# Two hybrid blocks on one core: first weight units split on VectorE, keys and queries by tile, squares of the post norms added on VectorE

## The chip, the cores and the metric

One core of one Trainium2 chip. The metric is the device time of one execution in microseconds (us); lower is better. Engines: PE (TensorE, matmuls), PEld (its weight loads), DVE (VectorE), ACT (ScalarE), POOL (GpSimd) and SP (SyncE, which here issues every DMA).

## What is computed

Two transformer-like blocks on a sequence of 512 tokens of width 1024, in f32, each with 16 meta tokens put in front. Reduced to what matters:

```python
def rmsnorm(x, g):
    return x * lax.rsqrt(jnp.mean(x * x, axis=-1, keepdims=True) + 1e-6) * g

# first block
mix = hybrid_mixer(rmsnorm(h, norm_mix_pre))      # retention + stick-breaking attention, gates, w_out
h = h + rmsnorm(mix, norm_mix_post)
h = h + rmsnorm(swiglu(rmsnorm(h, norm_ffn_pre)), norm_ffn_post)      # d_ff 2816
# second block
h = h + rmsnorm(mixer(rmsnorm(h, pre_mix_norm)), post_mix_norm)       # two convolutions, w_out
h = h + rmsnorm(swiglu_2(rmsnorm(h, pre_ffn_norm)), post_ffn_norm)
```

There are thus eight RMS norms, n = 0 to 7. The even ones (0, 2, 4, 6) are the norms ahead of a product, the odd ones (1, 3, 5, 7) the post norms.

## The kernel before, in words

**Layout.** Activations lie transposed: 8 tiles (k = 0 to 7) of 128 channels by 512 tokens, or 528 (FULL) with the meta tokens. Weights come in 140 units of 128x2048 f32 (1 MB), two buffers each of `w_raw`, `w_hi`, `w_lo`. For nearly f32 accuracy every operand is split in an fp32r part and a rest: ACT writes `w_hi` (a copy of `w_raw` to fp32r, `split_hi`, L872), DVE writes `w_lo` = `w_raw` - `w_hi` (`split_lo`, L1297), and each product is three matmuls (`mm3`, L477 to L481). A unit of kind P has 2 output strips of 8 tiles, R has 4 strips of 4, D has 8 strips of 2. A strip is a PSUM bank of 128x512; ACT or DVE takes it out and counts `strip_free`.

**Order of the work.** Each engine has one instruction stream, written out by hand, and waits on counting semaphores; there is no scheduler. SP issues the load of unit u when `w_hi` and `w_lo` of unit u-2 are there (`load`, L403). At the start it issues the four parts of h, unit 0, constants, unit 1, and the rotary table (L388 to L402). In w_out, the reload of h and `meta2` is issued ahead of the later units (L439, L440), once X_lo of the mixed rows is done.

**A norm (n)**: ACT squares the tiles into the two buffers of `sq` (`squares`, L907); PE sums over channels with a matmul by a matrix of ones, plain f32, into bank 6 (`sums`, L525 to L535), one per tile, each of them counted on `sq_added`; square k waits for sum k-2, since its buffer must be free; then ACT computes std as Ln and Exp (`norm`, L880). In a pre norm DVE then multiplies h by gain and std (`normed`, L1322), ACT writes X_hi, DVE X_lo (L1316; `norm_split`, L1309); in a post norm DVE makes `normed` from `acc` and adds it to h (`norm_add`, L1329).

- n = 1: phase w_out, 4 P units. PE puts two sums behind each of units 1, 2 and 3 and the last two at the end (`out_product`, L794). ACT splits the next weights (`split_hi`) ahead of the square of each odd tile (L1164); DVE copies each strip to `acc` and splits after each odd one (L1679).
- n = 3 and n = 7: phase ffn_end, one D unit. DVE adds each strip to `acc` (`add_up`, L1445); the 8 sums stand on PE behind the whole unit. With n = 3 ACT splits a weight unit ahead of the last square (L1206), and DVE makes its rest behind its last strip.
- n = 5: phase w_out2_b, two R units, sums behind both; ACT splits a unit ahead of squares 0 and 4 (L1282), DVE makes both rests behind its last strip.
- After most sums PE runs `keep_warm`: matmuls of ones by ones whose result nobody reads.

**The start.** PE: sums of norm 0, 36 matmuls of `keep_warm`, then `key_strip` (L568): the keys' strip of unit 0, tile by tile as X_lo comes, then 16 small matmuls for the meta tokens, then the queries' strip of the same unit (`unit(at, 0, 0, "P", SEQ, from_x, [1])`, L703). ACT copies unit 0 to `w_hi` between the second and third X_hi (`first_hi(0)`, L902), unit 1 after the small operands of the first quad (L1042). DVE makes the rest of unit 0 behind its second `normed` (L1324) and of unit 1 behind the norm. Then come K_hi and K_lo, the meta keys KM, Q_hi and Q_lo, and with these the first scores (L588).

## Time and profile before

| | |
|---|---|
| time, median of 3 runs | 2011.96 us (2009.48 to 2012.11) |
| time of the profiled execution | 2012.64 us |
| its span, first to last instruction | 2010.8 us |
| busy: PE / PEld / DVE / ACT / POOL | 1948.0 / 1644.5 / 1102.2 / 714.0 / 19.1 us |
| mean granted TensorE clock (share of 2.4 GHz) | 0.992 |
| weights and inputs read from HBM | 154.48 MB |

Busy time of PE is a model: matmuls are pipelined, so a matmul's duration is longer than its step, the distance from one start to the next. In a timeline, the time in square brackets is how long the engine had stood idle before an instruction, and who ended it. An f32 matmul appears as two records. L870 is the line of ACT's helper for every activation, so its instructions are told apart by their tiles; L1307 is the same for DVE's scalar_tensor_tensor.

### The profile page before, as it was taken

What the parts mean: (1) busy time and instruction counts of PE and PEld (TensorE: products, weight loads), DVE (VectorE), ACT (ScalarE), POOL (GpSimd) and SP (SyncE); (2) the same over time, 40 slices, a digit from 0 to 9 for tenths busy, and PEclk for the clock granted to TensorE, in tenths of its full rate; (3) what the DMA queues carried; (4) which work ended last, traced back from release to release, by engine and by line L of the source; (5) the groups of instructions that cost most, each with busy time, mean ns of one, the idle gap of its engine ahead of it and who ended that gap; (6) DMA issues with size and microseconds to landing.
All of it is one profiled execution on the core that took longest, in us unless ns stands there. A gap on an engine that the chain in (4) does not pass through costs nothing.

```text
span 2010.8 us, 25243 instructions
## 1 busy us (share of the span) xinstructions
PE 1948.0 (97%) x10194; PEld 1644.5 (82%) x10194; DVE 1102.2 (55%) x1354; ACT 714.0 (36%) x853; POOL 19.1 (1%) x16
## 2 busy tenths in 40 slices
PE   7999999899999999999999999999999999999996
PEld 6988989789888898978768888886998668888884
DVE  4556565542463736357364544546699664544545
ACT  5666666522323233233342222224333442222222
POOL 1000000000000000000000000000000000000000
PEclk9999999899999999999999999999999999999998
DMA  4011111032222121212412323222121112323221
GB/s 160 33 42 43 63 42 43 21 115 78 80 84 87 70 73 63 84 66 82 149 62 85 104 83 104 90 97 84 64 85 63 63 62 85 104 83 104 89 99 42
DMA packets 23474, 157.53 MB, mean 78 GB/s; under 512 B 2672, under 2 KB 3056, under 8 KB 5360
## 3 DMA queue, kind: packets, MB, share of 16 engines
q1 hardware_dynamic: 23408, 156.59, 22.5%
q8 instruction: 49, 0.80, 0.2%
q14 instruction: 17, 0.14, 0.0%
HBM read 154.48 MB, written 2.10 MB: 78 GB/s over the span
## 4 chain that ended last, share of the span: by engine, by line
PE 84%; DVE 8%; ACT 4%; issue 2%; DMA 1%; DVEq 0%; SPq 0%; ACTq 0%
PE psum L479 27%; PE psum L480 26%; PE psum L481 26%; PE psum L609 2%; PE psum L533 2%; DVE z L1307 2%; DVE normed L1307 2%; DVE h L1336 1%; ACT w_hi L870 1%; DVE w_lo L1300 1%; ACT std L870 1%; DMA w_raw<-in_units 0%; ACT sp L870 0%; PE psum L630 0%; ACT X_hi L870 0%
## 5 line engine op out<-in xcount | busy, mean ns | idle before, releaser
L479 PE MATMUL psum<-X_hi,w_hi 128*128 128x512 f32 (+1 forms) x1632 | 601.9, 369 | 5.9 <-DVE X_lo L1316 5.0
L481 PE MATMUL psum<-X_hi,w_lo 128*128 128x512 f32 (+1 forms) x1632 | 595.0, 365 | 0.0
L480 PE MATMUL psum<-X_lo,w_hi 128*128 128x512 f32 (+1 forms) x1632 | 594.9, 365 | 0.0
L870 ACT ACTIVATE w_hi<-w_raw 128x2048 fp32r<-128x2048 f32 x140 | 267.4, 1910 | 411.9 <-PE psum L481 395.4
L1300 DVE TENSOR_TENSOR w_lo<-w_raw,w_hi 128x2048 fp32r<-128x2048 f32 x138 | 316.0, 2291 | 144.5 <-ACT w_hi L870 144.5
L479 PEld LDWEIGHTS psum<-X_hi,w_hi 128*128 128x128 f32 x1632 | 306.5, 188 | 64.2 <-issue 6.7
L480 PEld LDWEIGHTS psum<-X_lo,w_hi 128*128 128x128 f32 x1632 | 306.9, 188 | 49.0 <-issue 2.2
L481 PEld LDWEIGHTS psum<-X_hi,w_lo 128*128 128x128 f32 x1632 | 306.5, 188 | 49.0
L1449 DVE TENSOR_TENSOR acc<-acc,psum 128x512 f32<-128x512 f32 x216 | 142.1, 685 | 82.0 <-PE psum L481 82.0
L479 PE MATMUL psum<-M_hi,w_hi 128*128 128x512 f32 x352 | 136.9, 389 | 0.0
L480 PE MATMUL psum<-M_lo,w_hi 128*128 128x512 f32 x352 | 136.9, 389 | 0.0
L481 PE MATMUL psum<-M_hi,w_lo 128*128 128x512 f32 x352 | 136.9, 389 | 0.0
L479 PE MATMUL psum<-w_hi,X_hi 128*128 128x256 f32 x448 | 126.5, 282 | 0.0
L481 PE MATMUL psum<-w_hi,X_lo 128*128 128x256 f32 x448 | 126.3, 282 | 0.0
L480 PE MATMUL psum<-w_lo,X_hi 128*128 128x256 f32 x448 | 126.3, 282 | 0.0
L1696 DVE TENSOR_TENSOR silu_a<-silu_a,psum 128x512 f32<-128x512 f32 x44 | 30.3, 688 | 133.1 <-ACT silu_a L870 133.1
L1702 DVE TENSOR_TENSOR silu_a<-silu_a,psum 128x512 f32<-128x512 f32 x44 | 30.3, 688 | 120.3 <-PE psum L481 120.3
L479 PEld LDWEIGHTS psum<-w_hi,X_hi 128*128 128x128 f32 x448 | 85.8, 192 | 0.4
L480 PEld LDWEIGHTS psum<-w_lo,X_hi 128*128 128x128 f32 x448 | 85.6, 191 | 0.4
L481 PEld LDWEIGHTS psum<-w_hi,X_lo 128*128 128x128 f32 x448 | 85.7, 191 | 0.0
L870 ACT ACTIVATE silu_a<-psum 128x512 f32<-128x512 f32 x44 | 26.4, 599 | 166.9 <-PE psum L481 166.8
L533 PE MATMUL psum<-sq,ones 128*128 128x512 f32 (+1 forms) x160 | 68.1, 556 | 15.8 <-ACT sq L870 15.8
(241 smaller groups left out, 2606.8 us busy)
## 6 DMA issues: line engine op xcount, KB each, us to landing
w_raw<-in_units SPq DMA_DIRECT2D x140, 1024.0 KB, 4.8
h<-in_xfm SPq DMA_DIRECT2D x4, 528.0 KB, 6.6
h<-in_xfm SPq DMA_DIRECT2D x1, 2112.0 KB, 7.5
decay<-in_dec SPq DMA_DIRECT2D x4, 512.0 KB, 4.6
out<-h SPq DMA_DIRECT2D x4, 512.0 KB, 2.8
rot<-in_consts SPq DMA_DIRECT2D x1, 528.0 KB, 11.6
acc<-in_consts SPq DMA_DIRECT2D x1, 448.0 KB, 9.1
vec<-in_vecs SPq DMA_DIRECT2D x1, 108.0 KB, 3.5
```

The costliest lines, as they stand in the source:

```text
L479: nc.tensor.matmul(dst, w2[0], x2[0], start=first, stop=False, skip_group_check=True)
L480: nc.tensor.matmul(dst, w2[0], x2[1], start=False, stop=False, skip_group_check=True)
L481: m = nc.tensor.matmul(dst, w2[1], x2[0], start=False, stop=last, skip_group_check=True)
L533: m = nc.tensor.matmul(psum[:, 6 + hf, 0:b - a], ones[:, :], sq[:, k % 2, a:b], start=k == 0, stop=k == DT - 1, skip_group_check=True)
L609: m = nc.tensor.matmul(psum[:, 4 + KEY_BANK[b], c0:c0 + KEY_LEN[b2]], cmat[:, C_TRI if b2 == b else C_ALL, :], x[:, KEY_OFF[b2]:KEY_OFF[b2 ...
L870: return nc.scalar.activation(out_, in_, f, **kw)
L1300: v.tensor_tensor(w_lo[at.ring(j)][:, :], w_raw[at.ring(j)][:, :], as_f32(w_hi[at.ring(j)][:, :]), ALU.subtract).then_inc(w_lo_ready, 1)
L1307: return v.scalar_tensor_tensor(out=out_, in0=in0, scalar=scalar, in1=in1, op0=op0, op1=op1)
L1336: v.tensor_tensor(h[:, k, META:FULL], h[:, k, META:FULL], normed[:, k % 2, 0:SEQ], ALU.add)\
L1449: v.tensor_tensor(dst[:, m, :], dst[:, m, :], strip_view(at.bank(s + n), SEQ), ALU.add)\
L1696: v.tensor_tensor(silu_a[:, c, :], silu_a[:, c, :], strip_view(at.bank(s + c), SEQ), ALU.mult)\
L1702: v.tensor_tensor(silu_a[:, c, :], silu_a[:, c, :], strip_view(at.bank(s + 2 + c), SEQ), ALU.mult)\
```

## The change

- **Start, weights.** `first_split` on DVE replaces `first_hi` on ACT and `first_lo` on DVE: DVE waits for units 0 and 1, copies each to `w_hi` and subtracts, before it begins norm 0. PE runs 20 matmuls of `keep_warm` ahead of the sums and 24 behind them.
- **Start, strips.** In the first `key_strip`, after tile k of the keys comes tile k of the queries, for k up to 6; then key tile 7, the 16 small matmuls, and query tile 7.
- **Post norms.** ACT writes the square of tile 0 to `sq_sum` (the first 512 columns of `normed`); DVE adds the squares of tiles 1 to 6 to it (`add_squares`), each behind the next strip's copy or add; PE has two matmuls by ones (`post_sums`): of `sq_sum` and of the square of tile 7. `split_hi` comes behind the square of its tile, not ahead of it.

```diff
@@ -252,6 +252,7 @@
     normed = sb("normed", [P, 2, FULL])
+    sq_sum = normed[:, 0, 0:SEQ]
     meta2_f = sb("meta2_f", [P, DT, META])
@@ -534,6 +535,16 @@
+        def post_sums(n):
+
+            pe.wait_ge(std_ready, 2 * n - 1)
+            pe.wait_ge(sq_added, DT * n + DT - 2)
+            nc.tensor.matmul(psum[:, 6, :], ones[:, :], sq_sum, start=True, stop=False,
+                             skip_group_check=True).then_inc(sq_added, 1)
+            pe.wait_ge(sq_done, DT * (n + 1))
+            nc.tensor.matmul(psum[:, 6, :], ones[:, :], sq[:, (DT - 1) % 2, 0:SEQ], start=False, stop=True,
+                             skip_group_check=True).then_inc(sq_added, 1)
+
         def keep_warm(n, bank=5):
@@ -541,8 +552,9 @@
         pe.wait_ge(ones_ready, 1)
+        keep_warm(20)
         sums(0, FULL)
-        keep_warm(36)
+        keep_warm(24)
         def split(hi, lo, *ix):
@@ -570,10 +582,16 @@
             w = [ring3(r[at.ring(j)], "P") for r in (w_hi, w_lo)]
+
+            def queries(k, sig):
+                mm3(psum[:, at.bank(s + 1), :], [y[:, k, P:2 * P] for y in w], from_x(k, META, FULL),
+                    k == 0, k == DT - 1, sig)
             for k in range(DT):
                 mm3(psum[:, at.bank(s), :], [y[:, k, 0:P] for y in w], from_x(k, META, FULL), k == 0, k == DT - 1)
+                if first and k < DT - 1:
+                    queries(k, None)
             if first:
@@ -584,6 +602,8 @@
             m.then_inc(strip_done, 1)
+            if first:
+                queries(DT - 1, (strip_done, 1))
@@ -700,7 +720,6 @@
         key_strip(at, 0, 0, counted(x_lo_ready, 0), True)
-        unit(at, 0, 0, "P", SEQ, from_x, [1])
         pe.wait_ge(cmat_ready, 1)
@@ -796,9 +815,7 @@
                 unit(at, j, 2 * j, "P", SEQ, x, None, ready if j == 0 else None)
-                if j:
-                    sums(n, SEQ, range(2 * j - 2, 2 * j))
-            sums(n, SEQ, range(DT - 2, DT))
+            post_sums(n)
@@ -828,7 +845,7 @@
         ffn("", 0)
-        sums(3, SEQ)
+        post_sums(3)
         keep_warm(16)
@@ -856,12 +873,12 @@
                  counted(y2_ready, CT) if j == 0 else None, j == 0)
-        sums(5, SEQ)
+        post_sums(5)
         keep_warm(16)
         ffn("_2", 1)
-        sums(7, SEQ)
+        post_sums(7)
@@ -881,7 +898,10 @@
             for k in range(DT):
-                if DT * n + k >= 2:
+                if n % 2:
+                    if k >= 3:
+                        act.wait_ge(sq_added, DT * n + k - 2)
+                elif DT * n + k >= 2:
                     act.wait_ge(sq_added, DT * n + k - 1)
@@ -898,25 +918,22 @@
                 for k in range(DT):
-                    if k == 2 and n == 0:
-                        first_hi(0)
                     act.wait_ge(norm_scaled, DT * n + k + 1)
-        def squares(n, tile, width, ready):
+        def squares(n, tile, width, ready, then=None):
             def src(k):
                 ready(k)
-                a(sq[:, k % 2, 0:width], tile(k), ACT.Square).then_inc(sq_done, 1)
+                dst = sq_sum if n % 2 and k == 0 else sq[:, k % 2, 0:width]
+                a(dst, tile(k), ACT.Square).then_inc(sq_done, 1)
+                if then:
+                    then(k)
             return src
                                        "sigmoid": "sigmoid_and_others"}[functions])
-
-        def first_hi(u):
-            act.wait_ge(w_loaded[u], 16)
-            a(w_hi[u][:, :], w_raw[u][:, :], ACT.Copy).then_inc(w_hi_ready, 1)
@@ -1039,7 +1056,6 @@
               as_f32(y[:, :, 0:32]).unsqueeze(2).broadcast_to([P, DT, 2, 32]), ACT.Copy).then_inc(quad_ready, 1)
-        first_hi(1)
         key_hi(0, at, 0, 0)
@@ -1161,13 +1177,11 @@
-            def ready(k):
+            def next_weights(k):
                 if k % 2:
-                    strips(at, k)
                     split_hi(at, k // 2)
-                act.wait_ge(strip_free, at.strip(k) + 1)
-
-            norm(n, squares(n, lambda k: acc[:, k, :], SEQ, ready), SEQ)
+            norm(n, squares(n, lambda k: acc[:, k, :], SEQ,
+                            lambda k: act.wait_ge(strip_free, at.strip(k) + 1), next_weights), SEQ)
@@ -1203,14 +1217,14 @@
-            def ready(k):
-                at = Place("ffn_end" + tag, depth=4)
+            at = Place("ffn_end" + tag, depth=4)
+
+            def next_weights(k):
                 if n == 0 and k == DT - 1:
-                    strips(at, k)
                     split_hi(at, 0)
-                act.wait_ge(strip_free, at.strip(k) + 1)
             m = 4 * n + 3
-            norm(m, squares(m, lambda k: acc[:, k, :], SEQ, ready), SEQ)
+            norm(m, squares(m, lambda k: acc[:, k, :], SEQ,
+                            lambda k: act.wait_ge(strip_free, at.strip(k) + 1), next_weights), SEQ)
@@ -1279,13 +1293,13 @@
-        def ready(k):
-            at = Place("w_out2_b")
-            if k % 4 == 0:
-                strips(at, k + 3)
+        at = Place("w_out2_b")
+
+        def next_weights(k):
+            if k % 4 == 3:
                 split_hi(at, k // 4)
-            act.wait_ge(strip_free, at.strip(k) + 1)
-        norm(5, squares(5, lambda k: acc[:, k, :], SEQ, ready), SEQ)
+        norm(5, squares(5, lambda k: acc[:, k, :], SEQ,
+                        lambda k: act.wait_ge(strip_free, at.strip(k) + 1), next_weights), SEQ)
         norm(6, squares(6, lambda k: h[:, k, META:FULL], SEQ, lambda k: act.wait_ge(post_done, 2 * DT + k + 1)), SEQ, 3)
@@ -1320,8 +1334,6 @@
                     ALU.mult, ALU.mult).then_inc(norm_scaled, 1)
-                if k == 1 and n == 0:
-                    first_lo(0)
                 if k:
@@ -1336,16 +1348,25 @@
-        def first_lo(u):
+        def first_split(u):
+            dve.wait_ge(w_loaded[u], 16)
+            v.tensor_copy(w_hi[u][:, :], w_raw[u][:, :]).then_inc(w_hi_ready, 1)
             dve.wait_ge(w_hi_ready, u + 1)
+        def add_squares(n, k):
+            dve.wait_ge(sq_done, DT * n + k + 1)
+            if k > 1:
+                dve.wait_ge(sq_added, DT * n + k - 1)
+            v.tensor_tensor(sq_sum, sq_sum, sq[:, k % 2, 0:SEQ], ALU.add).then_inc(sq_added, 1)
+
+        for u in range(2):
+            first_split(u)
         dve.wait_ge(vec_in, 16)
         norm_split(0, 0, FULL, "pre_mix")
-        first_lo(1)
         dve.wait_ge(consts_in, 16 * 3)
@@ -1442,12 +1463,14 @@
-        def add_up(dst, at, s, ms):
+        def add_up(dst, at, s, ms, norm=None):
                     .then_inc(strip_free, 1)
+                if norm and m > 1:
+                    add_squares(norm, m - 1)
@@ -1676,15 +1699,17 @@
-        def out_product(phase):
+        def out_product(phase, n):
             at = Place(phase).four()
                 v.tensor_copy(acc[:, m, :], strip_view(at.bank(m), SEQ)).then_inc(strip_free, 1)
+                if m > 1:
+                    add_squares(n, m - 1)
                 if m % 2:
-        out_product("w_out")
+        out_product("w_out", 1)
         dve.wait_ge(x_loaded, 32)
@@ -1729,7 +1754,7 @@
             at = Place("ffn_end" + tag, depth=4)
-            add_up(acc, at, 0, range(DT))
+            add_up(acc, at, 0, range(DT), 4 * n + 3)
             if n == 0:
@@ -1858,7 +1883,7 @@
         dve.wait_ge(strip_free, at.strip(0))
-        add_up(acc, at, 0, range(DT))
+        add_up(acc, at, 0, range(DT), 5)
         for j in range(2):
```

## Rows read from the trace of the kernel before

**Rows 1.** The page: busy time of PE; the group of the norm sums.
```profile
PE 1948.0 (97%) x10194; PEld 1644.5 (82%) x10194; DVE 1102.2 (55%) x1354; ACT 714.0 (36%) x853; POOL 19.1 (1%) x16
...
L533 PE MATMUL psum<-sq,ones 128*128 128x512 f32 (+1 forms) x160 | 68.1, 556 | 15.8 <-ACT sq L870 15.8
```

**Rows 2.** Timeline of w_out: start us, us, engine line op out<-in [idle before<-releaser].
```profile
973.24 1.92 ACT L870 ACTIVATE w_hi<-w_raw 128x2048 fp32r<-128x2048 f32 x1 [8.20 <-DMA w_raw<-in_units]
...
974.99 1.88 PE L533 MATMUL psum<-sq,ones 128*128 128x512 f32 x4
...
977.54 0.50 PE L479 MATMUL psum<-X_hi,w_hi 128*128 128x512 f32 x1 [0.67 <-DVE w_lo L1300]
...
988.37 0.39 PE L481 MATMUL psum<-X_hi,w_lo 128*128 128x512 f32 x1
...
988.60 1.88 PE L533 MATMUL psum<-sq,ones 128*128 128x512 f32 x4
...
990.54 0.40 PE L480 MATMUL psum<-X_lo,w_hi 128*128 128x512 f32 x1
...
1001.24 2.86 PE L533 MATMUL psum<-sq,ones 128*128 128x512 f32 x6
...
1005.10 2.29 DVE L1300 TENSOR_TENSOR w_lo<-w_raw,w_hi 128x2048 fp32r<-128x2048 f32 x1 [2.97 <-ACT w_hi L870]
...
1008.27 0.75 DVE L1307 SCALAR_TENSOR_TENSOR normed<-acc,vec,std 128x512 f32<-128x512 f32 x1 [0.88 <-ACT std L870]
```

**Rows 3.** Timeline of DVE at norm 3 (ffn_end).
```profile
1377.84 2.48 DVE L1449 TENSOR_TENSOR acc<-acc,psum 128x512 f32<-128x512 f32 x4
...
1384.56 0.69 DVE L1449 TENSOR_TENSOR acc<-acc,psum 128x512 f32<-128x512 f32 x1 [0.67 <-PE psum L481]
...
1394.12 0.22 DVE L1738 COPY h<-meta_f 128x128 f32<-128x128 f32 x1
...
1395.06 0.75 DVE L1307 SCALAR_TENSOR_TENSOR normed<-acc,vec,std 128x512 f32<-128x512 f32 x1 [0.72 <-ACT std L870]
```

**Rows 4.** Timeline of DVE at norm 5 (w_out2_b).
```profile
1601.12 0.69 DVE L1449 TENSOR_TENSOR acc<-acc,psum 128x512 f32<-128x512 f32 x1 [2.03 <-PE psum L481]
...
1611.55 0.75 DVE L1307 SCALAR_TENSOR_TENSOR normed<-acc,vec,std 128x512 f32<-128x512 f32 x1 [3.50 <-ACT std L870]
```

**Rows 5.** Timeline of the last norm, DVE and ACT.
```profile
1987.85 0.69 DVE L1449 TENSOR_TENSOR acc<-acc,psum 128x512 f32<-128x512 f32 x1 [0.67 <-PE psum L481]
...
1995.10 0.69 ACT L870 ACTIVATE std<-psum,vec 128x512 f32<-128x512 f32 x1 [1.22 <-PE psum L533]
```

**Rows 6.** The start: timeline; DMA issues 6.0 to 6.9 us; busy time and PEclk, 44 to 50.
```profile
6.26 0.44 SPq L400 DMA_DIRECT2D w_raw<-in_units  x1
...
w_raw<-in_units SPq DMA_DIRECT2D x1, 1024.0 KB, 10.8
...
15.58 8.20 PE L541 MATMUL psum<-ones 128*128 128x128 f32 x72
...
17.29 1.45 DVE L1307 SCALAR_TENSOR_TENSOR normed<-h,vec,std 128x528 f32<-128x528 f32 x2 [17.29 <-ACT std L870]
...
23.45 0.70 DVE L1316 TENSOR_TENSOR X_lo<-normed,X_hi 128x528 fp32r<-128x528 f32 x1
...
31.98 1.50 DVE L1316 TENSOR_TENSOR X_lo<-normed,X_hi 128x528 fp32r<-128x528 f32 x2
...
36.04 0.47 PE L479 MATMUL psum<-X_hi,w_hi 128*128 128x512 f32 x1
...
40.16 1.40 DVE L1406 TENSOR_TENSOR K_lo<-psum,K_hi 64x512 fp32r<-64x512 f32 x2
...
42.62 0.29 DVE L1420 TENSOR_TENSOR KM_lo<-KM,KM_hi 128x128 fp32r<-128x128 f32 x1 [0.37 <-ACT KM_hi L870]
...
44.08 0.47 PE L479 MATMUL psum<-Q_hi,K_hi 128*128 128x512 f32 x1 [2.31 <-DVE Q_lo L1307]
...
44.00:50.00 6.00, 5.92 (x30) 5.59 (x31) 2.29 (x1) 3.33 (x6) 0.00 (x0) 0.72 0.34 97
```

## What I expect of the change, before seeing its time

> **What bounds the kernel now.** I read the page first: PE is busy 97% of the span [rows 1]. So time is won only where PE's instruction stream gets shorter, or in the few places where PE stands waiting. Those places are the start (one weight split and the first norm) and the eight norms. I therefore went to the timeline of the start and of each post norm (n = 1, 3, 5, 7; where norm n's sums are 8 matmuls by `ones`), and there followed back what ended the last wait before the norm's first VectorE instruction. Everything between the norms is PE at its step of 0.23 us per 512-column matmul (988.37 to 988.60, [rows 2]); if a norm ends earlier, all that follows moves with it.
>
> An f32 sum over 512 columns is two records, 0.43 us each: from the first of four records at 988.60 to the second matmul of the next unit at 990.54 are 1.94 us, less one step of 0.23 is 1.71 us for two sums, 0.86 us for one [rows 2]. In all, 80 sums are the 160 records of the page [rows 1]; the change takes away 6 of each 8 in four norms.
>
> **Part C, n = 1 (w_out), 3.1 us.** Before, two sums stand on PE after each of units 1, 2 and 3.
> - After unit 1 (974.99) nothing is won. Unit 2 starts at 977.54 and was released by w_lo, whose w_hi had waited for a DMA until 973.24 [rows 2]. That DMA is queued on SP behind the reload of h, which the change doesn't touch. PE just idles 2.5 us instead of 0.7.
> - After unit 2: 1.71 us off PE's stream, whole.
> - After unit 3 (T = 1001.24): now the last add of a strip is followed by the VectorE add of squares and ACT's last square in parallel, then two sums. The copy of strip 7 starts at T+0.2 and takes 0.69, the add the same, so the first sum starts at T+1.6, the two sums take 1.7+0.3 to the end of the last record, and Ln begins at T+3.6 (before: T+5.6). But ACT now puts w_hi behind the last square: 0.9+0.65, then 1.92, then w_lo 2.29, which VectorE runs before the norm. The norm's first instruction comes at T+5.7. It stood at 1008.27 = T+7.0 [rows 2]. Gain 1.35. What is late next is thus w_lo, not the sums.
>
> Sum 1.71+1.35 = 3.1.
>
> **n = 3 (ffn_end), 4.0 us.** Before, the third square waits for a sum that PE only reaches after the whole unit, so squares and sums run one by one after the last strip. VectorE gets two 0.60 us instructions per strip (four adds back to back take 2.48, [rows 3]) where PE makes a strip in 1.36 (0.69 of add after 0.67 of waiting for PE, [rows 5]). It starts late, at 1377.84, because of a w_lo, and with the adds of squares it wins back only 0.16 per strip: I lay the eight strips out one by one and get the last strip's add at 1385.3 instead of 1384.56. The last add of squares ends 1386.6, the two sums and Ln follow at 1388.7. The w_hi after the last square is done at 1388.6, w_lo 2.2 later, the small copy 0.2: norm at 1391.05 against 1395.06 [rows 3]. Again w_lo decides, by 0.8 us, which covers the lag of the strips.
>
> **n = 5 (w_out2_b), 4.8 us.** Strips take 2.7 us, so VectorE has room. Last add 1601.12 [rows 4], last square done 1602.5, w_hi 1604.4, w_lo(0) in its shadow, w_lo(1) 1604.5 to 1606.8: norm at 1606.75 against 1611.55 [rows 4].
>
> **n = 7 (end), 3.85 us.** No weights here. Last add 1987.85; add of squares to 1989.15; two sums; Ln at 1991.25 against 1995.10 [rows 5]. VectorE has 1.36 us per strip for 1.2 us of work, and it starts this unit without a lag. If each instruction cost its full 0.69 plus a semaphore (1.4 to 1.5 per strip), it would lag about 1 us at the end; that is the lower bound, 2.8.
>
> The norms in between (2, 4, 6) keep their 8 sums; I cost them at nothing.
>
> **Parts A and B (the start), 3.9 us.** Before, ACT and VectorE split unit 0 in the middle of the norm: first norm instructions 17.29, first X_lo only 23.45, last X_lo ends 33.48 [rows 6]. After: VectorE is in order and now waits for w_raw1 before its norm. That load is issued at 6.26 and lands 10.8 us later, at 17.06 [rows 6], so the std, ready at 17.2 before, no longer decides. Then a copy of 128x2048 and a subtraction of 2.29. The trace has no such copy on VectorE. Nearest rows: a 128x128 copy takes 0.22 [rows 3], a 128x128 subtraction 0.29 [rows 6]; if some 0.16 is fixed (my estimate from 2.29 for 2048 and 0.29 for 128, about 1.04 ns a column), the copy costs about half per column, so 1.2 us. The other bound is the subtraction's own 2.29. I take 1.2, since it is the same operation. The norm starts at 20.6; two norm instructions (1.45), then the run from 23.45 to 33.48 (10.03) repeats: last X_lo at 32.1, 1.35 earlier (0.3 earlier with the slow copy).
> The Trainium skill (VectorE: DVE Perf Modes, Mode 2x_2P) says that a one-source f32 copy within SBUF uses both read ports and makes two results a cycle while tensor_tensor can't; its table gives 1224 ns for 2048 elements at that rate. By it the sum is the one above; with the rate of the subtraction it is 1.1 us less.
>
> B: tiles come every 1.42 us (23.45 to 31.98 is six of them). Six matmuls of a tile are 1.36 us, so the queries' 7 tiles vanish beside VectorE. The last two tiles come only 0.8 apart, so key tile 7 waits 0.7 for PE; then the 16 small matmuls, then the last query tile. Before, the keys' strip was done when the queries began, at 36.04, 2.56 after the last X_lo [rows 6]; now it is done 0.7 to 0.85 later, at X_lo+3.4, and the queries at X_lo+4.1. ACT no longer has 1.9 of w_hi before K_hi, VectorE no w_lo before K_lo. First K_hi half takes 0.6 to 0.7, so first K_lo at X_lo+4.15; from there to the scores it takes 44.08-40.16 = 3.92 [rows 6] as before. Scores at X_lo+8.07 = 40.2 instead of 44.08, gain 3.9; with the slow copy 2.8. POOL's memsets begin at the last X_lo as before and ended before 40, well ahead of the scores; cost nothing. If they decided, scores would still not start before X_lo+5. keep_warm: 72 records take 8.20 [rows 6]; 48 of them 5.5, from about 15 to 20.5, then PE idles until about 22.8 (before: 0.5). The 20 ahead of the sums push these back by up to 2 us, hidden since the norm waits for the weights.
>
> **Sum:** 3.9+3.1+4.0+4.8+3.85 = 19.65. The profiled execution took 2012.64 (span 2010.8 and 1.8 around it), 0.68 above the median of 2011.96. 2011.96-19.65 = 1992.3. I take 0.5 off the gain for the clock (next), 1992.8.
>
> **Rivals.**
> 1. *The clock falls in the new gaps.* After the 2.31 us gap before 44.08 the granted clock was 0.72 as a mean of 44 to 50 [rows 6], which is some 3.4 us at its lower level of 1.2 GHz and costs about 1.7 us. New gaps of like size: 20.5 to 22.8, the one before the scores now 4.0 us long, 974.99 to 977.5, and 2.1 us after ffn_end. Against: the waits of PE within w_out left its step at 0.23 us [rows 2], and a fall that begins within a gap costs less than one that begins behind it. Each fall costs up to 1.7 us; two or three cost 3 to 5: 1996 to 1998. Chance 0.22. The Trainium skill (TensorE: Matmul & The Clock Gate, HAM oscillation) warns of just this, waits that let the clock fall so that the next burst starts cold; the trace agrees at 44.08.
> 2. *The start gives nothing or loses*: w_raw1 lands later or the copy is slow, the clock falls at the first tile, and VectorE's head of line holds the norm; price 4 to 7 us: 1996.5 to 2000. Chance 0.08.
> 3. *More is won*: the low clock around 46 goes with the gap's new place, PE's sums in w_out count more: 1988 to 1991. Chance 0.12.
> 4. *Slower.* VectorE's adds make PE wait, so that the gaps grow and the clock stays low through the following units. At 1.2 GHz a microsecond gives back half; the gain of 19.65 is eaten when the low clock lasts over 39 us more in total. The only fall in these rows lasted 3.4 us, so twelve of them: 2013 or more. Chance 0.01.
> 5. *The sums were covered anyway* (true for unit 1 of w_out): then only the start counts, 2008; within 0.2% if that fails too. Chance 0.02, of which 0.01 no change. The 7.4 us from the last strip's add to Ln in norm 7 speaks against it [rows 5].
>
> **Numbers.** My forecast's own case (1991 to 1995.5) has 0.55. The range 1988.5 to 1998.5 takes in rivals 1 and 3 and most of 2. A measurement tells 0.2%, 4 us, from no change. Faster 0.98, same 0.01, slower 0.01.
>
> **What would show it.** L533 plus the new sum's lines: 160 records become 112. In w_out, unit 2 starts again on w_lo; unit 3 1.7 us earlier. Before norms 1, 3 and 5 the last wait of VectorE is on w_hi/w_lo, before norm 7 on std. First norm instruction near 20.6, a VectorE copy of 1.2 us, scores near 40. I am wrong if the copy takes 2.3, if the granted clock shows new 0.5 stretches, or if ffn_end's strip adds run over 1 us late.

## The result, and the profile after

| | before | changed |
|---|---|---|
| median of the timed runs, us | 2011.82 (2009.48 to 2012.11, 4 runs) | 1994.38 (1994.04 to 1994.88, 4 runs) |
| ratio, 95% interval | 1 | 0.9916 (0.9899 to 0.9933) |
| profiled execution: time, span, us | 2012.64, 2010.8 | 1994.37, 1992.6 |
| PE busy, us (records) | 1948.0 (10194) | 1927.8 (10162) |
| norm sums on PE (records) | 160 | 96 + 8 + 8 = 112 |

The forecast was 1992.8, the range 1988.5 to 1998.5. The page and the view of groups of the changed kernel, against [rows 1]:

```profile
PE 1927.8 (97%) x10162; PEld 1639.4 (82%) x10162; DVE 1118.2 (56%) x1380; ACT 711.1 (36%) x851; POOL 19.1 (1%) x16
...
L534 PE MATMUL psum<-sq,ones 128*128 128x264 f32 (+1 forms) x96 | 34.8, 483 | 8.0 <-ACT sq L887 8.0
...
L1362 DVE TENSOR_TENSOR normed<-normed,sq 128x512 f32<-128x512 f32 x24 | 16.4, 684 | 0.1
...
L542 PE MATMUL psum<-normed,ones 128*128 128x512 f32 x8 | 4.4, 630 | 6.5 <-DVE normed L1362 6.5
...
L545 PE MATMUL psum<-sq,ones 128*128 128x512 f32 x8 | 4.1, 592 | 0.0
```

PE lost 20.2 us of busy time, and VectorE took over 16.4 us in 24 adds with hardly any wait of its own (0.1 us). The span fell by 18.2.

**Where the 18.2 us lie.** I set the same instruction in both traces side by side; the difference of two rows is what has been won up to there.

| up to | before | changed | won in this stage | forecast |
|---|---|---|---|---|
| first strip copy of w_out | 963.63 | 959.98 | 3.65 (the start) | 3.9 |
| norm 1 | 1008.27 | 1002.91 | 1.71 | 3.1 |
| norm 3 | 1395.06 | 1385.53 | 4.17 | 4.0 |
| norm 5 | 1611.55 | 1597.18 | 4.84 | 4.8 |
| norm 7 | 1996.48 | 1978.24 | 3.87 | 3.85 |

**The start.** Timeline of the changed kernel (start, duration, engine, line, [idle before <- releaser]):

```profile
12.53 1.23 DVE L1353 CAST w_hi<-w_raw 128x2048 fp32r<-128x2048 f32 x1 [12.53 <-DMA w_raw<-in_units]
13.79 2.29 DVE L1355 TENSOR_TENSOR w_lo<-w_raw,w_hi 128x2048 fp32r<-128x2048 f32 x1
16.29 1.23 DVE L1353 CAST w_hi<-w_raw 128x2048 fp32r<-128x2048 f32 x1 [0.21 <-DMA w_raw<-in_units]
17.55 2.29 DVE L1355 TENSOR_TENSOR w_lo<-w_raw,w_hi 128x2048 fp32r<-128x2048 f32 x1
19.76 1.44 DVE L1321 SCALAR_TENSOR_TENSOR normed<-h,vec,std 128x528 f32<-128x528 f32 x2
...
29.78 1.51 DVE L1330 TENSOR_TENSOR X_lo<-normed,X_hi 128x528 fp32r<-128x528 f32 x2
...
34.42 0.47 PE L480 MATMUL psum<-X_hi,w_hi 128*128 128x512 f32 x1
...
39.24 0.76 PE L480 MATMUL psum<-Q_hi,K_hi 128*128 128x512 f32 x1 [3.88 <-DVE Q_lo L1321]
```

Busy time, PEclk, DMA share and GB/s of the same kernel in slices of 2 us, PE alone:

```profile
38.00:40.00 2.00, 0.76 (x2) 0.58 0.00 0
40.00:42.00 2.00, 2.00 (x9) 0.50 0.00 0
42.00:44.00 2.00, 2.00 (x11) 0.50 0.40 61
44.00:46.00 2.00, 2.00 (x11) 0.71 0.78 303
46.00:48.00 2.00, 2.00 (x19) 1.00 0.42 168
```

The unknown copy took 1.23 us: half of the subtraction's 2.29, not the same. The Trainium skill (VectorE: DVE Perf Modes, the perf-mode tier table) has 1227 ns for an f32 tensor_copy of 2048 elements within SBUF; this trace agrees. w_raw1 landed at 16.29 and not at 17.06 (SP issued its load at 5.26 instead of 6.26, and it took 11.0 us instead of 10.8), so the norm began at 19.76 and the scores at 39.24, 4.84 us before the 44.08 of [rows 6]. But they ran at 1.2 GHz: the clock fell in the 3.88 us in which PE waited for Q_lo, and was back only after 45. From the scores to the first value strip matmul it takes 45.03 - 39.24 = 5.79 us, where before it took 4.69. That gives 1.10 back, and 3.74 stay. The kernel before had a fall here too, but its first scores still ran at the full clock (PEclk 1.00 in 42 to 44, 0.82 in 44 to 46, 0.50 in 46 to 48).

**w_out.** Timeline, PE and then DVE:

```profile
971.11 0.39 PE L482 MATMUL psum<-X_hi,w_lo 128*128 128x512 f32 x1
973.96 0.80 PE L480 MATMUL psum<-X_hi,w_hi 128*128 128x512 f32 x1 [2.45 <-DVE w_lo L1314]
974.55 0.63 PE L481 MATMUL psum<-X_lo,w_hi 128*128 128x512 f32 x1
974.98 0.63 PE L482 MATMUL psum<-X_hi,w_lo 128*128 128x512 f32 x1
...
977.06 0.40 PE L481 MATMUL psum<-X_lo,w_hi 128*128 128x512 f32 x1
977.30 0.39 PE L482 MATMUL psum<-X_hi,w_lo 128*128 128x512 f32 x1
...
997.45 0.69 DVE L1706 COPY acc<-psum 128x512 f32<-128x512 f32 x1 [4.13 <-PE psum L482]
...
1000.70 2.29 DVE L1314 TENSOR_TENSOR w_lo<-w_raw,w_hi 128x2048 fp32r<-128x2048 f32 x1 [1.96 <-ACT w_hi L887]
1002.91 0.75 DVE L1321 SCALAR_TENSOR_TENSOR normed<-acc,vec,std 128x512 f32<-128x512 f32 x1
```

Unit 2 was again released by w_lo, and up to it nothing was won (13.91 us from the first strip copy before, 13.98 now). Its step is then 0.43 us (974.55 to 974.98) for the first six matmuls, and 0.23 only from 977.06. From unit 2's first matmul to the last strip's copy the time fell from 23.90 to 23.49: 0.41 us of the 1.71 that had been PE's sums. From that copy to the norm it fell from 6.83 to 5.46: 1.37. Directly ahead of the norm VectorE runs w_lo, without a gap between them, so w_lo decides and not std, which was ready at 1002.2.

**Norms 3, 5 and 7**, timeline of DVE, and ACT's Ln of norm 7:

```profile
1379.83 0.68 DVE L1470 TENSOR_TENSOR acc<-acc,psum 128x512 f32<-128x512 f32 x1
...
1383.07 2.29 DVE L1314 TENSOR_TENSOR w_lo<-w_raw,w_hi 128x2048 fp32r<-128x2048 f32 x1 [1.96 <-ACT w_hi L887]
...
1385.53 0.75 DVE L1321 SCALAR_TENSOR_TENSOR normed<-acc,vec,std 128x512 f32<-128x512 f32 x1
...
1592.78 4.49 DVE L1314 TENSOR_TENSOR w_lo<-w_raw,w_hi 128x2048 fp32r<-128x2048 f32 x2
1597.18 0.74 DVE L1321 SCALAR_TENSOR_TENSOR normed<-acc,vec,std 128x512 f32<-128x512 f32 x1
...
1976.86 0.69 ACT L887 ACTIVATE std<-psum,vec 128x512 f32<-128x512 f32 x1 [2.02 <-PE psum L545]
...
1978.24 0.75 DVE L1321 SCALAR_TENSOR_TENSOR normed<-acc,vec,std 128x512 f32<-128x512 f32 x1 [3.52 <-ACT std L887]
```

In norms 3 and 5 it is w_lo again that ends last, in norm 7 std. The last strip's add of ffn_end moved from 1384.56 [rows 3] to 1379.83, 0.63 less than norm 1 had moved: that is the lag of VectorE that the prediction put at 0.74.

### The profile page after: what moved, and what is told of

It is laid out like the page before. It is cut to its first block, busy times and chain, and to the rows that moved or that the text cites. A ratio compares the mean times of both kernels' runs of the same rounds, so it can differ in the third digit from the quotient of the medians.

```text
span 1992.6 us, 25210 instructions
## 1 busy us (share of the span) xinstructions
PE 1927.8 (97%) x10162; PEld 1639.4 (82%) x10162; DVE 1118.2 (56%) x1380; ACT 711.1 (36%) x851; POOL 19.1 (1%) x16
## 4 chain that ended last, share of the span: by engine, by line
PE 84%; DVE 9%; ACT 4%; issue 2%; DMA 1%; SPq 0%; DVEq 0%; ACTq 0%
PE psum L480 27%; PE psum L481 26%; PE psum L482 26%; PE psum L629 2%; DVE z L1321 2%; DVE normed L1321 1%; DVE w_lo L1314 1%; DVE h L1348 1%; ACT w_hi L887 1%; DMA w_raw<-in_units 1%; ACT sp L887 0%; PE psum L599 0%; PE psum L602 0%; ACT std L887 0%; PE psum L650 0%
## 5 line engine op out<-in xcount | busy, mean ns | idle before, releaser
L1321 DVE SCALAR_TENSOR_TENSOR z<-glu,vec,z 128x512 f32<-128x512 f32 x120 | 80.4, 743 | 0.0
```

Of the source, the lines that this page charges most:

```text
L1321: return v.scalar_tensor_tensor(out=out_, in0=in0, scalar=scalar, in1=in1, op0=op0, op1=op1)
```

## The experiments

Theory: the three parts add up, and what is missing against the sum was lost where the granted clock fell in PE's gaps. Rivals: the parts hinder each other (B needs A, or VectorE is overloaded), or the slow stretches have other causes (late operands, transfers). All ratios are to the kernel before, measured on the same chip in the same session (medians 2012.84, 2012.26 and 2012.64 in the three sessions). Each session had its own chip and fills four rows of the table, in this order. Of the three, only the second has the changed kernel. So where kernels of different sessions are compared by medians, a difference of 1 us is within what the kernel before itself moved (2011.82 to 2012.84).

| kernel | median, us (range) | ratio (95%) | span |
|---|---|---|---|
| C alone | 1997.52 (1996.14 to 1999.99) | 0.9929 (0.9915 to 0.9942) | 1995.0 |
| A + C | 1993.37 (1992.45 to 1995.96) | 0.9907 (0.9892 to 0.9922) | 1991.7 |
| B + C | 1999.23 (1997.29 to 2000.77) | 0.9932 (0.9918 to 0.9945) | 1997.6 |
| warm matmuls before the scores | 1994.97 (1990.00 to 1996.39) | 0.9909 (0.9895 to 0.9924) | 1988.9 |
| changed, again | 1994.03 (1993.30 to 1994.52) | 0.9908 (0.9892 to 0.9925) | 1992.2 |
| warm matmuls in w_out | 1994.21 (1992.90 to 1995.19) | 0.9908 (0.9891 to 0.9924) | 1993.4 |
| last w_lo behind the norms | 1990.80 (1987.13 to 1991.92) | 0.9887 (0.9871 to 0.9904) | 1989.8 |
| three edits, without B | 1990.33 (1988.96 to 1990.45) | 0.9888 (0.9872 to 0.9905) | 1988.7 |
| w_hi ahead of the square | 1992.55 (1990.63 to 1994.60) | 0.9898 (0.9881 to 0.9914) | 1992.8 |
| split of unit 1 behind norm 0 | 1991.82 (1990.56 to 1992.35) | 0.9895 (0.9879 to 0.9912) | 1990.5 |
| four edits, with B | 1986.86 (1986.63 to 1987.02) | 0.9872 (0.9856 to 0.9889) | 1985.2 |
| four edits, without B | 1989.78 (1988.93 to 1990.44) | 0.9888 (0.9871 to 0.9904) | 1987.5 |

### The parts, one by one

Without the interleaving (A + C):

```diff
-                if first and k < DT - 1:
-                    queries(k, None)
...
-            if first:
-                queries(DT - 1, (strip_done, 1))
...
         key_strip(at, 0, 0, counted(x_lo_ready, 0), True)
+        unit(at, 0, 0, "P", SEQ, from_x, [1])
```

> The changed kernel without the interleaving: VectorE splits the first two units, the queries' strip follows the keys' strip whole. My theory (clock): the queries' strip then fills the gap before the first scores; scores start at 40.9 instead of 39.2, but at the full clock, 2.9 us instead of 5.8, so the value strip starts at 43.8 instead of 45.0 and the run is about 1.3 us shorter than the changed kernel, 1993.1. Rival (hidden work): interleaving saves the 1.6 us by which the scores start earlier; then this run is 1.6 us longer, 1996.0.

C alone has in addition the split of the first two units as it was before. The cut shows the part on VectorE; w_hi of both units goes back to ACT, w_lo of unit 0 into the middle of the norm, and PE again runs 36 warm matmuls behind the sums and none ahead of them:

```diff
-        for u in range(2):
-            first_split(u)
         norm_split(0, 0, FULL, "pre_mix")
+        first_lo(1)
```

> The kernel before with the post-norm part alone (start as before). My theory: the parts add up. In the trace of the changed kernel the post norms and the w_out stage make up 14.5 of the 18.2 us of span (1.7 at w_out, 4.1 at norm 3, 4.8 at norm 5, 3.8 at norm 7), so 2011.8-14.5 = 1997.3 us, and unit 2 of w_out starts at the low clock here too. Rival (the start and the norms interact, for instance by where the low clock falls): more than 1 us away from 1997.3.

B + C has that second edit and keeps the interleaving.

> The changed kernel with the weights of the first two units split as before (ACT and VectorE in the middle of the norm, 36 warm matmuls behind the sums) but with the interleaving. My theory: K_lo still waits for the w_lo of unit 1, so the scores start at 44.1 as before; PE has a gap of over 6 us ahead of them and runs them all at the low clock: value strip at 49.9, total 1994.4+4.8 = 1999.2. Rival (the queries' 4.8 us leave PE's stream and this shows in the end): about 1994.4 to 1995.

C alone gave 1997.52, 15.3 us under the kernel before, and its profile has the first scores at 43.68. So C carries most of the gain, and as much as its stages gave in the changed kernel (1997.3 had been expected), although the clock did not fall in unit 2 of w_out, as the expectation had it. A is worth 4.2 us on top of C (the value strip starts at 44.12 instead of 48.38); A without C was not run. B is worth nothing as it is built: with it 1994.38 and 1994.03, without it 1993.37 (ranges that overlap; the medians alone don't settle its sign). The traces say why. A + C, timeline and slices of PE:

```profile
41.00 0.47 PE L480 MATMUL psum<-Q_hi,K_hi 128*128 128x512 f32 x1 [1.50 <-DVE Q_lo L1318]
```
```profile
40.00:42.00 2.00, 1.00 (x5) 1.00 0.00 0
42.00:44.00 2.00, 2.00 (x15) 1.00 0.04 8
```

Its scores start 1.76 us later than the changed kernel's, but behind a gap of 1.50 instead of 3.88 us; the clock stays up, and the value strip starts at 44.12. With the interleaving it starts at 45.03 (44.06 to 45.03 in the five profiles with this start). So the 1.8 us that the interleaving wins at the scores are given back by the value strip, to the clock behind its longer gap: all of them to within 0.1 us, or more.

B + C hit the expected total by two errors that cancel. Its value strip came at 47.88, not near 49.9: the scores began 0.9 us earlier than expected, at 43.21, and took 4.68 instead of 5.8 us, since part of the low clock lay in the 6.5 us gap ahead of them. And 2.0 us were then lost between there and w_out (last section). Against C alone its value strip is 0.5 us earlier; the 1.7 us by which its median is higher lie in that later stretch (1.6 us of it in the traces), not in the strips.

### The clock in the gap before the scores

```diff
         key_strip(at, 0, 0, counted(x_lo_ready, 0), True)
+        keep_warm(16)
         pe.wait_ge(cmat_ready, 1)
```

> The changed kernel with 16 more matmuls of ones by ones (3.7 us) in PE's gap between the last query tile and the first scores. My theory (clock): scores and meta scores then run at the full clock, 2.9 instead of 5.8 us; value strip at about 42.1 instead of 45.0, total 2.9 us less, 1991.5. Rival (the scores are slow for another reason, or the next waits take the gain): 1994.4, unchanged.

```profile
38.62 0.47 PE L480 MATMUL psum<-Q_hi,K_hi 128*128 128x512 f32 x1 [0.31 <-DVE Q_lo L1322]
```
```profile
40.00:42.00 2.00, 2.00 (x17) 1.00 0.00 0
42.00:44.00 2.00, 2.00 (x19) 1.00 0.34 61
```

Sixteen matmuls that compute nothing fill the gap, and the stretch from scores to value strip takes 3.13 us instead of 5.79: the value strip starts at 41.75, 2.4 us before that of A + C. So the mechanism is shown: with the gap filled the clock stays up, and B then is worth something. The timed median did not follow (1994.97, with runs from 1990.0 to 1996.4), though the profiled run, at a span of 1988.9, did. The two executions near 1990 had a mean granted clock of 0.994 and 0.995, the three at 1994.97 to 1996.39 one of 0.989 to 0.990. So what these lost went with more time at the low clock; where, has no profile.

### The changed kernel again, and warm matmuls in w_out

> The changed kernel once more, unaltered, so that the others of this group stand beside a second measurement and a second profile of it. Theory: what differs between its profiled executions is where the granted clock falls, not what is computed or waited for. So 1994.4 again within 1.5 us; the milestones up to the first rotated query strip move by under 0.3 us. What may differ is the stretch behind a gap of TensorE of 2.4 to 3.9 us: unit 2 of w_out and its neighbours take 23.5 us from its first matmul to the last strip's copy where the clock falls and 22.1 where it doesn't. Rival: the loss is tied to this program's own transfers or waits and returns in the same place with the same size, 23.5 us and 5.8 us from scores to value strip.

```diff
             for j in range(4):
+                if j == 2:
+                    keep_warm(10)
                 unit(at, j, 2 * j, "P", SEQ, x, None, ready if j == 0 else None)
```

> The changed kernel with ten matmuls of ones by ones (nothing reads their result) between the first two and the last two units of w_out, in the 2.45 us in which TensorE waits for w_lo. Theory (the clock falls in the gap): the first matmul of unit 2 comes at the same time, its step is 0.23 us from the start, unit 2 to the last strip's copy takes 22.1 instead of 23.5 us, and the kernel ends 1.4 us earlier in the executions in which the clock fell there: 1993.0 to 1994.4. Rival (unit 2 is slow because its operands or its buffers come late): 23.5 us again and 1994.4; if the ten are not done when w_lo is, up to 0.3 us later.

The changed kernel came back at 1994.03, with both falls in the same places (38 to 44 at 0.50, and unit 2 to last copy 23.70 us). So the figures of the rival came back (5.79 us from scores to value strip, and 23.70 for 23.5), and this run alone can't tell the clock from late operands; the warm matmuls can. Its milestones at the start moved more than I had said: scores at 38.52 instead of 39.24. With the warm matmuls, timeline and slices of PE, then DVE at norm 3:

```profile
974.98 0.50 PE L480 MATMUL psum<-X_hi,w_hi 128*128 128x512 f32 x1 [0.17 <-DVE w_lo L1316]
...
1380.93 1.88 PE L542 MATMUL psum<-normed,ones 128*128 128x512 f32 x2 [2.12 <-DVE normed L1364]
...
1386.01 0.75 DVE L1323 SCALAR_TENSOR_TENSOR normed<-acc,vec,std 128x512 f32<-128x512 f32 x1 [0.84 <-ACT std L889]
```
```profile
976.00:978.00 2.00, 2.00 (x10) 1.00 0.86 270
...
1382.00:1384.00 2.00, 2.00 (x3) 0.50 0.00 0
```

Unit 2 to last copy is 22.13 us, so unit 2 had been slow for its clock. Transfers are no cause: here 270 GB/s in 976 to 978 stand beside the full clock and the full pace, and in the changed kernel the slow slice 974 to 976 has only 61. The rival falls. In C alone, which has the gap but no fall (0.59 us busy and 1.00 in the slice 976 to 978), it is 22.09. But the total didn't move. Part of the gain went at once into a new fall: behind the 2.12 us gap at the end of ffn_end the clock dropped, the two sums took 1.88 and 1.91 us instead of 1.10 and 1.02, std came 1.6 us later against their start and took over from w_lo, and norm 1 to norm 3 grew from 382.62 to 383.44. All four kernels with these warm matmuls show a fall at this place, and none of the other ten profiles (before's among them) does. Why ten matmuls in w_out should bring it about 400 us later, I don't know.

### What ends last before the norms

Last w_lo behind the norms (here for norm 1; likewise in norms 3 and 5):

```diff
-                if m % 2:
+                if m % 2 and m < DT - 1:
                     split_lo(at, m // 2)
...
         norm_add(1, 0, "post_mix")
+        split_lo(Place("w_out"), DT // 2 - 1)
```

> The changed kernel with VectorE's last subtraction for the next weights (w_lo, 2.29 us) put behind the post norm instead of ahead of it, in norms 1, 3 and 5. Theory (w_lo decides when these norms start, by 0.6, 0.9 and 0.8 us before std): each norm starts right behind std, 2.3 us in all, 1992.1; the last wait of VectorE ahead of each norm is on ACT's std. Rival (the sums on TensorE decide, or the w_lo that is moved is then late for the unit behind it): 1994.4 or later.

```profile
1001.48 0.75 DVE L1321 SCALAR_TENSOR_TENSOR normed<-acc,vec,std 128x512 f32<-128x512 f32 x1 [3.60 <-ACT std L887]
...
1383.27 0.75 DVE L1321 SCALAR_TENSOR_TENSOR normed<-acc,vec,std 128x512 f32<-128x512 f32 x1 [3.45 <-ACT std L887]
...
1594.38 0.75 DVE L1321 SCALAR_TENSOR_TENSOR normed<-acc,vec,std 128x512 f32<-128x512 f32 x1 [1.32 <-ACT std L887]
```

From the last copy to norm 1: 4.89 instead of 5.46 us; norm 1 to norm 3: 381.79 instead of 382.62; last add to norm 5: 4.81 instead of 5.61. These are 0.57, 0.83 and 0.80, 2.2 us in the trace, and the median fell by 3.2. All three norms now wait for std. That w_lo had decided is shown. The w_lo behind the norm makes nobody late that the trace shows: from norm 5 to norm 7 it is 381.07 us, and 381.06 in the changed kernel.

w_hi ahead of the square, as before the change (in norm 5 the two splits now stand ahead of squares 3 and 7, before the change ahead of 0 and 4; not shown in the cut: ACT first waits for the strip):

```diff
             def src(k):
+                if then:
+                    then(k)
                 ready(k)
                 dst = sq_sum if n % 2 and k == 0 else sq[:, k % 2, 0:width]
                 a(dst, tile(k), ACT.Square).then_inc(sq_done, 1)
-                if then:
-                    then(k)
```

> The changed kernel with ACT's w_hi for the next unit ahead of the square of the same strip in the post norms, as before the change. Rival one (w_lo decides the norm's start, and it follows w_hi): w_hi comes some 0.75 us earlier, so norms 1, 3 and 5 start up to 0.6, 0.9 and 0.8 us earlier and the kernel ends 1 to 2.3 us earlier, 1992 to 1993. Rival two (the last square, and with it the sums and std, now wait for 1.9 us of w_hi): std moves by 1.9 less the 0.8 us that the square waited for VectorE's copy anyway, so it becomes the later one, and each of the three norms starts about 0.5 to 1 us later: 1996 to 1997, with the last wait ahead of the norms on std. I hold with the second.

```profile
1003.46 0.75 DVE L1324 SCALAR_TENSOR_TENSOR normed<-acc,vec,std 128x512 f32<-128x512 f32 x1 [0.88 <-ACT std L887]
...
1385.66 0.75 DVE L1324 SCALAR_TENSOR_TENSOR normed<-acc,vec,std 128x512 f32<-128x512 f32 x1 [0.73 <-ACT std L887]
...
1597.36 0.75 DVE L1324 SCALAR_TENSOR_TENSOR normed<-acc,vec,std 128x512 f32<-128x512 f32 x1
```

I had held with the second rival, and was wrong. std does take over in norms 1 and 3, but it comes at a time that is still before the old w_lo: last copy to norm 1 is 5.17 (5.46), norm 1 to norm 3 is 382.20 (382.62), and in norm 5, where two w_lo stand back to back, 5.61 both ways. So 0.7 us is won. In norm 1 the last square starts 1.87 us after VectorE's last copy, instead of 0.79. But std is ready only 0.27 us later (5.05 instead of 4.78 after that copy), because the square's sum on PE had stood 0.9 us behind the other one anyway, and std had 0.7 us to spare. The order that the change chose for ACT is no gain of its own. The median is 1.5 us lower, with overlapping ranges and from another session.

### VectorE's head of line at the start

```diff
-        for u in range(2):
-            first_split(u)
+        first_split(0)
         norm_split(0, 0, FULL, "pre_mix")
+        first_split(1)
...
-        keep_warm(24)
+        keep_warm(16)
...
         query_hi(0, at, 1)
+        act.wait_ge(w_hi_ready, 2)
```

> The changed kernel with VectorE's split of the second weight unit behind the first norm instead of ahead of it (16 instead of 24 warm matmuls behind the sums, so that these don't run into the first tile). Theory: the norm's start is set by VectorE's own queue (19.76 us, after w_raw1's landing at 16.3 and 3.5 us of split) while std is ready at 16.1; unit 1 isn't needed before the value strip, and VectorE is idle for 4.0 us behind the last X_lo, in which the 3.5 us of split fit. So norm at 16.1 to 16.3, first scores at 35.7 instead of 39.2, 3.5 us won: 1990.9. Rival one: ACT's constants or the memsets decide when the scores start, so 1 us is won or less. Rival two: the split behind the norm delays K_lo and so the scores by up to 3.5 us, nothing is won: 1994.4.

```profile
17.12 1.45 DVE L1322 SCALAR_TENSOR_TENSOR normed<-h,vec,std 128x528 f32<-128x528 f32 x2 [1.71 <-ACT std L887]
...
28.57 1.22 DVE L1354 CAST w_hi<-w_raw 128x2048 fp32r<-128x2048 f32 x1
29.83 2.29 DVE L1356 TENSOR_TENSOR w_lo<-w_raw,w_hi 128x2048 fp32r<-128x2048 f32 x1
32.69 1.41 DVE L1428 TENSOR_TENSOR K_lo<-psum,K_hi 64x512 fp32r<-64x512 f32 x2 [0.57 <-ACT K_hi L887]
...
36.60 0.77 PE L480 MATMUL psum<-Q_hi,K_hi 128*128 128x512 f32 x1 [3.88 <-DVE Q_lo L1322]
```

The split fits between the last X_lo and K_lo with 0.57 us left, and the norm waits for std alone. std was ready at 17.0 in this execution instead of 16.1, so 2.64 us were won at the scores and not 3.5; the median is 1991.82, 2.2 to 2.6 below the changed kernel's. So in part A as built, the wait for w_raw1 and its split ahead of the norm cost 1.9 to 2.6 us at the scores (against 38.52 and 39.24 in the two profiles of the changed kernel). This profile also has the longer stretch of the last section.

### Put together

Three edits without B (the last w_lo behind the norms, warm matmuls in w_out):

> Three edits to the changed kernel at once: keys and queries strips one after the other as before, the ten matmuls of ones within w_out, and the last w_lo behind the norms. Theory: they act in different places and add up: 1.0 us (measured alone before), 0 to 1.4 and 2.3 us, so 1989.7 to 1991.1. Rival (whatever is won ahead of a norm is given back behind it, since the next unit's weights decide): 1993.4, what the first of the three gave by itself.

The same and the split of unit 1 behind the norm:

> The changed kernel with four edits: split of unit 1 behind the norm, last w_lo behind the norms, warm matmuls within w_out, and keys and queries strips one after the other instead of interleaved, without the warm matmuls ahead of the scores. Theory: split of unit 1 behind the norm takes 3.5 us off the 1990.3 of the same kernel without it: 1986.8. Rival: with the strips one after the other K_lo is wanted 0.8 us earlier, while VectorE is still busy with the split of unit 1, but the queries strip of 5.5 us covers that; if it doesn't, 0.8 us less is won: 1987.6.

Four edits with B (split of unit 1, last w_lo, both sets of warm matmuls):

> The changed kernel with four edits: split of unit 1 behind the norm, last w_lo behind the norms, warm matmuls ahead of the scores (16) and within w_out (10). Theory: they add up, from one profiled execution: 3.5 + 2.2 + about 2.5 at the start (the low clock behind the gap cost that much in the profiles) + 1.4 = 9.6, so about 1985; at the least the first two, 1988.7, if the clock then falls elsewhere. Rival: the warm matmuls only move the fall of the clock to later places, 1988 to 1990.

```profile
36.45 0.47 PE L480 MATMUL psum<-Q_hi,K_hi 128*128 128x512 f32 x1 [0.31 <-DVE Q_lo L1325]
...
968.61 0.50 PE L480 MATMUL psum<-X_hi,w_hi 128*128 128x512 f32 x1 [0.27 <-DVE w_lo L1318]
...
1374.02 1.64 PE L542 MATMUL psum<-normed,ones 128*128 128x512 f32 x2 [2.13 <-DVE normed L1366]
```

The first came to 1990.33, as the sum said. The second should have been 3.5 lower and is 0.6: its value strip stood at 41.20, 2.67 us earlier, but at the first copy in w_out only 1.1 was left; the 1.6 us went where the last section has it. The third is at 1986.86, 7.2 to 7.5 us under the changed kernel and 25.8 under the one before, every one of four runs within 0.4 us: the lowest of all. Its value strip starts at 39.57, 1.6 us ahead of the second's, which is B's worth with its gap covered. It lies between my two figures (1985 and 1988.7): against last w_lo alone, norm 1 to norm 3 is 383.21 instead of 381.79, the fall behind ffn_end again.

## Why the prediction was right, and where not

- **What bounds the kernel**: right. The span fell by what five places gave, and between them nothing moved by more than the clock's doing.
- **The start, 3.9**: 3.74 at the value strip. That this is so near is luck, for two errors offset each other: w_raw1 landed 0.77 us earlier than the one row I had, having been issued 1.0 us earlier, which put the scores at 39.24 and not at 40.2, and the low clock after the gap lasted longer, which took 1.1 back. The gap of 4.0 us had been foreseen (3.88), and its price under rival 1.
- **n = 1, 3.1**: 1.71. The step that failed is "after unit 2: 1.71 us off PE's stream, whole". The sums after unit 1, put at nothing, had done something after all: they filled the wait for w_lo. Without them PE stood for 2.45 us, the clock fell, and unit 2 gave 1.3 of the 1.7 back. The prediction had this gap, at 2.5 us, and listed it under rival 1, but its argument against, that PE's waits in w_out had left the step at 0.23, came from a wait of 0.67 us. In C alone, where the clock happened to hold, the term came out whole (22.09 against 23.90, 1.81), and with the gap filled as well (22.13). The other term (1.35) measured 1.37.
- **n = 3, 5, 7: 4.0, 4.8, 3.85**: 4.17, 4.84 and 3.87. w_lo decides the first two (shown by moving it), std the last. VectorE's lag was 0.63 against 0.74.
- **Rival 1** came true in two of its four places, before the scores and in w_out: 0.5 us had been taken off for it, and 1.1 + 1.3 would have been right. The Trainium skill's warning (TensorE: Matmul & The Clock Gate, HAM oscillation) that waits let the clock fall and the next burst starts cold is what these two places of the changed kernel show. At 44.08 of the kernel before, which the prediction names for it, the burst started at the full clock and lost it some 1.2 us later. Rivals 2, 4 and 5 are out; of 3, nothing. (The 7.4 us that rival 5 cites are 7.25 by its own rows, 1995.10 - 1987.85; nothing hangs on it.)
- **Sum**: 19.65 - 0.5 = 19.15 forecast, 18.2 measured in the traces and 17.4 between the medians. The median is 1.6 us above the forecast: 0.9 for gain that didn't come, and 0.7 because the profiled execution of the kernel before had stood 0.68 above its median and that of the changed kernel stood on it.

## What to carry to other kernels

Work that is "hidden in a wait" on PE may be what holds its clock up: before you take it away, look how long the bare gap gets, and price the 1.2 GHz stretch behind it (here 1.4 us in w_out, and 2.7 us at the scores, 5.79 against 3.13, of which the kernel before already paid 1.6) like any other term. Where an engine is in order, ask for each item ahead of the critical one who needs it first: both single edits that beat the changed kernel clearly (medians 3.2 and 2.2 to 2.6 us lower, ranges apart) only put a weight split behind a norm instead of ahead of it. And a gain of one microsecond in a kernel with such gaps is read from traces, stage by stage; the median of five runs doesn't show it.

## Not expected

**The clock falls in fixed places, but for how long is another matter in each execution.** In slices of 4 us, PEclk is under 0.97 in the same few spots and nowhere else in all 14 profiles (before the last unit): the first scores, 96 to 116, 376 to 404, unit 2 of w_out, and (with warm matmuls in w_out only) behind ffn_end, each at a gap of PE of some 1.8 to 4 us (6.5 in B + C). The kernel before has the first three too, at 44 to 52, 104 to 112 and 384 to 400. Adding (1 - PEclk) x 4 us over these slices up to the last unit gives an upper bound of what PE lost: 8.4 us in the kernel before, 11.9 in the changed one (11.9 again in its second profile), 8.5 in C alone, 6.8 with warm matmuls before the scores, 15.2 in B + C, 8.6 in the best. So of the 21.7 us (18.2 + 3.5) by which the rest got shorter, at most 3.5 went to the clock.

**From the value strip to the first copy in w_out the same instructions take one of two times**: 914.7 to 915.3 us in nine profiles, and 916.6 to 917.0 in five (B + C, warm matmuls in w_out, w_hi ahead of the square, split of unit 1 behind, four edits without B). In the five the fall at 376 to 404 amounts to 6.8 us by the same sum, in the nine to between 3.4 and 5.2. None of these edits touches that stretch. The traces, laid side by side, lose the 2 us in two places, each right behind a fall. From the value strip to a 1.4 us gap of PE (at 182.9 in the changed kernel) it takes 137.7 to 138.0 us in eight of the nine and 138.6 to 138.9 in the five (139.1 in C alone, which gets most of it back at its shorter fall near 390). From there to the 2.2 us gap at 392 all but C alone take 209.3 to 209.5. From that gap to the first copy it is 567.6 to 567.8 in the nine and 568.6 to 568.7 in the five. Around 100 the same sum is 3.4 us in each of the five and 1.7 in seven of the nine. So the 2 us go with more time at the low clock. What such time costs also depends on how much of it falls into PE's own waits: the three edits without B have 3.4 around 100 too, and are only 0.2 us late there. Several of the comparisons above, the combination of four edits without B among them, were decided by this 2 us and not by their edit. What makes the clock stay low longer in some executions stays open.

**The same gap doesn't always end the same.** The clock fell at a gap of 2.45 us before unit 2 in the changed kernel, and at 2.0 to 2.3 us in six others, while in C alone (2.2) and with warm matmuls before the scores (3.14 us) it held at 1.00. The gap behind ffn_end is 2.1 us in all thirteen profiles with part C, and the clock fell there in four. The length of the gap alone doesn't say whether the clock falls.
